# Moving the gate-logit copies and the preparation order in the latent attention of a decoder layer

## The reference

```python
q = split_heads(rms_norm(c_q, mla_cq_norm) @ mla_w_uq, MLA_HEADS)
kv = split_heads(rms_norm(c_kv, mla_ckv_norm) @ mla_w_ukv, MLA_HEADS)
...
q = rms_norm(q, mla_q_norm)
k = rms_norm(k, mla_k_norm)
q = concat(q[..., :64], rope(q[..., 64:], cos, sin))
k = concat(k[..., :64], rope(k[..., 64:], cos, sin))
o_mla = merge_heads(block_causal_attention(q, k, v)) @ w_branch_mla
g_fox, g_mla = split(sigmoid(gate_logit + b_gate))   # gate_logit = u @ w_in[:, gates], 1024 x 2048
return (g_fox * o_fox + g_mla * o_mla) @ w_out
```

## Time and profile before

| | |
|---|---|
| median of three runs | 2518.46 us |
| the profiled execution: its time | 2510.72 us |
| its span, first to last instruction | 2508.9 us |
| TensorE busy | 2383.4 us, 95% |
| TensorE weight loads busy | 2111.5 us, 84% |
| VectorE busy | 1411.8 us, 56% |
| ScalarE busy | 959.7 us, 38% |
| GpSimd busy | 505.7 us, 20% |
| mean granted TensorE clock | 0.973 of full speed |

### The profile page before, as it was taken

How to read it: one execution, slowest core, us unless ns; L and a number is a source line. 1 busy time by engine, 2 the same in 40 slices (tenths; PEclk the granted TensorE clock), 3 DMA queues, 4 the chain that set the end, 5 groups by cost and what they waited for, 6 DMA issues and landing times. The chain is left out here.

```text
span 2508.9 us, 36863 instructions
## 1 busy us (share of the span) xinstructions
PE 2383.4 (95%) x14060; PEld 2111.5 (84%) x14060; DVE 1411.8 (56%) x2057; ACT 959.7 (38%) x1621; POOL 505.7 (20%) x632
## 2 busy tenths in 40 slices
PE   7999999999978999989999999989999999999999
PEld 7999999999968878878777778778877888887887
DVE  8655655565554675573455555444286665556553
ACT  6333333343334444543343333353343333334332
POOL 0033300000022442430233333332401322000000
PEclk9999999999989999999899999989999999999999
DMA  5465632475321000000111111033614666327653
GB/s 193 143 208 190 215 114 104 161 274 184 136 84 52 26 2 25 26 20 30 38 37 38 42 37 37 31 118 134 227 59 134 226 204 203 130 71 287 205 200 105
DMA packets 132698, 297.99 MB, mean 119 GB/s; under 512 B 10096, under 2 KB 57072, under 8 KB 129216
## 3 DMA queue, kind: packets, MB, share of 16 engines
q1 hardware_dynamic: 132544, 295.88, 34.0%
HBM read 206.99 MB, written 88.72 MB: 118 GB/s over the span
## 5 line engine op out<-in xcount | busy, mean ns | idle before, releaser
L1079 DVE TENSOR_TENSOR f_w_lo<-f_rw,f_w_hi 128x1024 fp32r<-128x1024 f32 x154 | 194.7, 1265 | 224.1 <-ACT f_w_hi L591 224.1
L842 PE MATMUL f_ps<-u_hi,f_w_hi 128*128 128x260 f32 (+1 forms) x1056 | 280.8, 320 | 10.3 <-DVE u_lo L1017 10.1
L842 PE MATMUL f_ps<-u_lo,f_w_hi 128*128 128x260 f32 (+1 forms) x1056 | 281.0, 321 | 0.0
L842 PE MATMUL f_ps<-u_hi,f_w_lo 128*128 128x260 f32 (+1 forms) x1056 | 280.4, 320 | 0.0
L842 PE MATMUL f_ps<-f_far_hi,f_w_hi 128*128 128x260 f32 (+1 forms) x792 | 214.1, 325 | 20.1 <-DVE f_w_lo L1079 9.2
L591 ACT CAST f_w_hi<-f_rw 128x1024 fp32r<-128x1024 f32 x154 | 160.9, 1046 | 162.8 <-PE f_ps L842 159.0
L842 PE MATMUL f_ps<-f_far_hi,f_w_lo 128*128 128x260 f32 (+1 forms) x792 | 212.6, 323 | 0.0
L842 PE MATMUL f_ps<-f_far_lo,f_w_hi 128*128 128x260 f32 (+1 forms) x792 | 212.5, 323 | 0.0
L842 PEld LDWEIGHTS f_ps<-u_hi,f_w_hi 128*128 128x128 f32 x1056 | 176.3, 190 | 25.9 <-issue 11.3
L842 PEld LDWEIGHTS f_ps<-u_lo,f_w_hi 128*128 128x128 f32 x1056 | 176.3, 190 | 14.0
L842 PEld LDWEIGHTS f_ps<-u_hi,f_w_lo 128*128 128x128 f32 x1056 | 175.8, 190 | 13.6
(11 more groups left out here) (392 smaller groups left out, 5970.3 us busy)
## 6 DMA issues: line engine op xcount, KB each, us to landing
f_rw<-in_gu SPq DMA_DIRECT2D x88, 512.0 KB, 4.1
f_rw<-kept_dsum SPq DMA_DIRECT2D x32, 704.0 KB, 4.7
f_rw<-kept_hid SPq DMA_DIRECT2D x33, 520.0 KB, 5.4
f_rw<-in_down SPq DMA_DIRECT2D x24, 704.0 KB, 4.1
f_rw<-kept_hid SPq DMA_DIRECT2D x33, 512.0 KB, 5.5
h_in<-in_wd SPq DMA_DIRECT2D x11, 1024.0 KB, 6.8
kept_dsum<-h_in SPq DMA_DIRECT2D x44, 256.0 KB, 3.2
h_out<-in_wd SPq DMA_DIRECT2D x11, 1024.0 KB, 7.0
```

The source lines that it names most:

```text
L842: last = nc.tensor.matmul(out[:, b, 0:N], w[:, c], u[:, b * N:(b + 1) * N], start=(j < 3 and k == 0 and i == 0), stop=(k == 3 and i == 2), ...
L1079: nc.vector.tensor_tensor(slot(w_lo, st), src, slot(w_hi, st).bitcast(F32), ALU.subtract).then_inc(wlo_done, 1)
```

## The change

The copy of a block of logits moves by a step (from steps 2, 5, 9, 12 to 3, 6, 10, 13) and from behind the spread to ahead of the exponential. The groups are laid out anew, still 32: one fewer at place 1 of steps 0 and 1, one more at place 1 of step 2 and at place 0 of step 13. In the lead-in `split_hi` of the previous unit goes from behind the root to ahead of the square.

```diff
         GROUPS = {(w, x): 1 for w in range(14) for x in range(2)}
-        GROUPS.update({(0, 1): 2, (1, 1): 2, (3, 1): 2, (4, 1): 2, (11, 1): 2, (12, 1): 2, (13, 0): 0, (13, 1): 0})
+        GROUPS.update({(2, 1): 2, (3, 1): 2, (4, 1): 2, (6, 1): 1, (11, 1): 2, (12, 1): 2, (13, 1): 0})
-        COPY_AT, HI_AT, LO_AT = (2, 5, 9, 12), {3: 2, 4: 3, 10: 0, 11: 1}, {4: 2, 5: 3, 11: 0, 12: 1}
+        COPY_AT, HI_AT, LO_AT = (3, 6, 10, 13), {3: 2, 4: 3, 10: 0, 11: 1}, {4: 2, 5: 3, 11: 0, 12: 1}
...
                 for w in range(NW):
                     if more:
                         split_hi(p, h + 1, w - 3)
+                        copy_logits(p, h + 1, w)
                     exponential(p, h, w)
                     if more:
                         square(p, h + 1, w)
                         spread(p, h + 1, w - 1)
-                        copy_logits(p, h + 1, w)
                         root(p, h + 1, w)
...
             for w in range(NW):
+                split_hi(0, 0, w - 1)
                 square(0, 0, w)
                 root(0, 0, w)
-                split_hi(0, 0, w - 1)
                 copy_logits(0, 0, w, COPY_FIRST)
```

## The result

The changed kernel took 2550.74 us in the median of four runs (2547.32 to 2552.47), the kernel before 2517.89 us on the same chip (2510.72 to 2520.79). The ratio is 1.0133, with an interval of 1.0109 to 1.0157, so the change costs about 33 us. The forecast was 2541 us, with a range of 2521 to 2556. The profiled execution of after, one more than these four, took 2543.42 us, with a span of 2541.6. Before, the profiled one is among the four: 2510.72 us, with a span of 2508.9. Each is the fastest run of its kernel here, so the two can be set side by side.

The account below looks back on a forecast made before the run. TensorE was taken to set the pace in the heads. Terms 12.6 + 0.7 + 5.9 + 6.8 + 1.7 = 27.7 us gave 2538.4 from the profiled 2510.72, 2546.2 from the median; 2541 was taken, range 2521 to 2556.

Parts of the forecast that it names:

- The stall of step 3: TensorE's ninth group waits for the copy on ScalarE: 2.0 us in six heads, 0.6 in head 0, together 12.6.
- nothing comes back later: In the heads, the later wait hangs on sums and roots behind the stall, so none of the 2.0 us is regained.
- Rival (b): Step 3 has no stall because the root starts sooner; only the lead-in costs, 2517 to 2524 us; chance 0.13.
- Step 6: The group's stall for the copy hides in the broadcast's 1.14 us wait for GpSimd, with 0.3 to spare; cost 0.
- The wait left for L2320: Sign in step 6: the wait for GpSimd's last root step shrinks to some 0.3 us.
- Rival (c): Faster: the copy leaves ScalarE's stretch before step 5's root, step 6's wait goes, 9.4 us saved, 2501 to 2509; chance 0.05.
- The first weight loads: Steps 10 and 13: a group's first matmul takes 0.50 us behind a wait against 0.40 without; 0.7 in seven heads.
- The lead-in: Squares wait for the previous unit's high part, making five units later: 5.9 us, plus 1.7 for one clock loss.
- The waits stand at the sums: Sign in the lead-in: TensorE's sum L2502 waits for the squares, about 2.5 us ahead of units 1 and 3.
- The clock in the heads: Behind six stalls of 2.0 us the clock falls two times in three: four losses of 1.7, 6.8 us.
- The rival (d): Much slower: lower clock through the lead-in and a half-clock spell per head's stall, 36 us, 2547 to 2555; chance 0.10.

Follow-up runs that it names:

- heads-only kernel: The changed kernel with the lead-in's old order, high part behind the root again; 2536.46 us, ratio 1.0086 to the kernel before.
- groups behind the copy: The changed kernel with the old lead-in order and the two groups at place 1 of step 3 moved to step 4; 2528.01 us, ratio 1.0053.
- the lead-in alone: The kernel before with only the lead-in's new order, high part ahead of the square; 2522.29 us, ratio 1.0048.

## Why the prediction was right

**The stall of step 3.** Said: 2.0 us in six heads and 0.6 in the first. Measured: 1.93 to 1.97, and 0.52. The finish in a later step took 1.4 us off it, the high part behind the copy 0.4. This part stands as it was worked out. So does, within 0.1 us, the sentence that nothing comes back later: in the heads-only kernel a head with the clock held was 1.83 longer. Rival (b) needed the root to come sooner by the copy that was gone; the root waited 0.49 longer for VectorE instead.

**Step 6.** Said: hidden in the wait for the root, at 0. Measured: 5.01 us from broadcast to broadcast in both kernels. The wait left for L2320 was said to be some 0.3 and was 0, since TensorE's stall was nearly as long as the one that it covers. That it is a cover was shown from the other side, where two groups more in its place, taken from later steps, brought 1.3 us a head. Rival (c) needed a broadcast that comes earlier. The wait for L2320 did vanish, as it said, but only because TensorE stood still ahead of it: the broadcast came no earlier.

**The first weight loads.** Said: 0.1 a head. Head 0, whose clock held, grew by 0.88, of which the stall is 0.52. That leaves 0.36 for this and all else, three tenths more than said; it was not taken apart. In step 10 of head 1 the term is there: the load waits 0.16 us for the copy, the first matmul takes 0.49 and the next follows 0.32 behind it, where it was 0.40 and 0.24 before. But 0.50 is no sign of a wait by itself. The group at 1295.39 in the earlier trace rows also reads 0.50, behind the product and with no wait.

**The lead-in.** Said: 5.9 us, and 1.7 for a loss of clock. Measured: 5.7 in after and 6.6 alone, the clock in it. The waits stand at the sums, as said (2.21, 2.38 and 1.81 us for the squares of the k units). The mean clock of the stretch went from 0.86 to 0.84, but TensorE has room there, and most of that term wasn't paid.

**The clock in the heads.** This is the term that was mis-sized. Said: four losses of 1.7 us, 6.8. A head with the stall at full clock is 1.83 above before. Taking that away from heads 1 to 6 leaves 25.4 - 6 x 1.83 = 14.4 us. A plain loss was sized well: heads 1, 2, 3 and 5 have 1.5 to 1.8 each. What was too small is their number and the length of some. Every one of the six heads had at least one spell (head 5 at step 6, behind a wait of 1.03, not at step 3), head 4 had two (3.1 us), and the one of head 6 went on for 10 us (4.9). The rival (d), where each head's stall costs a spell, is thus half true: its bound for the clock was 17 with the lead-in, the heads took 14.4. The total came nearer than this term by errors of the other sign: the stalls and the lead-in came out 3.5 us smaller than forecast.

**What the sum doesn't hold.** 5.5 us lie ahead of the changed code, where the clock from 780 to 1150 us was 0.97 before and 0.94 after, and 4.6 of the other sign in head 7. Both are differences between single executions of the same instructions. In the ten profiles here the first product comes at 1169.76 to 1178.68 us, with the same instructions ahead of it, and the kernel before has the earliest; head 7 took 23.2 us in seven of the ten. So neither number belongs to the change. They nearly cancel, so that 32.7 measured against 27.7 forecast comes down to the clock in the heads (+7.6), the stalls in heads 1 to 6 (11.0 against 12.6, -1.6), the lead-in (-1.9) and 0.9 of the rest. The forecast of 2541 lies 10 under the median, since it was also anchored at the fastest of the runs of before.

## What to carry to other kernels

Before tying a wait to an instruction of another engine, sum what stands ahead of that instruction on its engine, and set it against where the waiting engine is by then; that sum was right to 0.1 us here, and it also names the mend (move what stands ahead, not the waiting work). Where a wait is already there, put independent work into it rather than another wait. On a TensorE that is otherwise full, price each new stall near 2 us at about twice its length (25.4 us for six stalls of 1.95 us here), because the granted clock fell behind most of them, and look for the same spell elsewhere before booking a gain.

## What the runs showed of the hardware

The clock fell to its lower level behind 5 of 6 stalls of 1.93 to 1.97 us in after; behind one it held, and in the heads-only kernel it held behind two of six (heads 1 and 4). Behind 1.5 us it held in 4 of 6. Behind two waits of 0.5 and 1.0 in a head it held in nearly all (5 of 6 heads with the finish later). In the kernel with groups behind the copy, the two waits of 0.73 and 0.67, 1.8 us apart, were followed by a loss in four heads of six. So in these runs no length of a single wait decides.

The wait of about 1 us in step 6 shows the same. As a wait for the root, 1.06 to 1.14 us, it was followed by no loss in the 14 heads of the kernel before and of the lead-in alone. As a wait for the copy, 0.96 to 1.05 us, with another wait in step 3 15 to 20 us ahead of it, it was followed by one in 2 of 7 heads of after and 5 of 7 of the heads-only kernel. Whether the earlier wait or the wait's own new place makes the difference stays open.

Most spells cost 1.5 to 1.8 us and a few three times as much, behind equal stalls. Kernels that have no changed line ahead of 1150 us had a mean clock of 0.93 to 0.97 between 780 and 1150 us, and head 7, at 23.2 to 27.8 us, went with its clock too. Single runs of the kernel before lie up to 18 us apart, and over 34 of them the time follows the mean clock of the run: 2506 to 2510 us at 0.975, 2519 to 2526 at 0.965 and 0.966. That is why a difference of some 10 us between two profiles has to be placed in a stretch before it is given a cause.
